# Twelve modulation blocks move from TensorE to VectorE, joined with a new order of work around them, in a two-layer encoder kernel

## What is computed

```python
for l in range(2):
    mod = c_act @ w_mod[l] + b_mod[l]          # (1024,) @ (1024, 6144)
    sh1, sc1, g1, sh2, sc2, g2 = split(mod, 6)
    h = rmsnorm(x, norm1_g[l]) * (1 + sc1) + sh1
    q, k, v, ca, cb, su, gates = split(h @ w_in[l])      # 5376 columns
    y_attn = sliding_window_attention(rope(q), rope(k), v) @ w_attn_o[l]
    y_conv = silu(layernorm(depthwise_conv31(ca * sigmoid(cb)))) @ conv_pw_w[l]
    y_ssm  = s5_ssm(su, ...)                   # (y @ glu_a) * sigmoid(y @ glu_b)
    mixed = gate_a * y_attn + gate_c * y_conv + gate_s * y_ssm
    x = x + g1 * (mixed @ w_out[l])
    h2 = rmsnorm(x, norm2_g[l]) * (1 + sc2) + sh2
    f_gate, f_up = split(h2 @ w_ffn_in[l])     # 2 x 2816 columns
    x = x + g2 * ((silu(f_gate) * f_up) @ w_ffn_out[l])
return rmsnorm(x, final_norm_g)
```

## Time and profile before

| | before |
|---|---|
| median of 3 runs (lowest, highest) | 977.05 us (977.03, 977.75) |
| the profiled execution's own time | 977.47 us |
| its span, first to last instruction | 975.6 us |
| TensorE busy | 926.7 us (95%) |
| VectorE busy | 669.4 us (69%) |
| ScalarE busy | 462.7 us (47%) |
| GpSimd busy | 9.4 us (1%) |
| mean granted TensorE clock | 0.990 |
| DMA, mean over the span | 201 GB/s |

### The profile page before, as it was taken

How to read it: one execution, slowest core, us unless ns; L and a number is a source line. 1 busy time by engine, 2 the same in 40 slices (tenths; PEclk the granted TensorE clock), 3 DMA queues, 4 the chain that set the end, 5 groups by cost and what they waited for, 6 DMA issues and landing times.

```text
span 975.6 us, 16235 instructions
## 1 busy us (share of the span) xinstructions
PE 926.7 (95%) x6917; PEld 783.7 (80%) x6917; DVE 669.4 (69%) x913; ACT 462.7 (47%) x540; POOL 9.4 (1%) x11
## 2 busy tenths in 40 slices
PE   5989999989999999999999999899999899999994
PEld 2888876667678888899989997567777799999994
DVE  4883999998567765473556758999947754444545
ACT  4684147624545565544445223574274544343432
POOL 2000000000000000000000000000000000000000
PEclk9999999999999999999999999899999999999998
DMA  8984356668696466566667334556869545555521
GB/s 356 237 266 138 112 187 215 216 183 306 268 283 216 153 224 223 199 210 230 209 173 210 120 106 173 179 190 192 297 228 331 180 173 195 174 189 199 173 87 43
DMA packets 128630, 196.13 MB, mean 201 GB/s; under 512 B 30793, under 2 KB 90705, under 8 KB 122415
## 3 DMA queue, kind: packets, MB, share of 16 engines
q1 hardware_dynamic: 128247, 195.03, 60.1%
q10 hardware_dynamic: 312, 0.08, 0.0%
HBM read 194.02 MB, written 1.06 MB: 200 GB/s over the span
## 4 chain that ended last, share of the span: by engine, by line
PE 53%; DVE 29%; ACT 7%; issue 5%; DMA 4%; SPq 2%; ACTq 0%; DVEq 0%
PE bank L569 15%; PE bank L570 15%; PE bank L571 15%; DVE wlo L1395 8%; DVE yc L1680 7%; DMA raw<-in_w_mod 3%; ACT whi L1062 3%; PE bank L607 2%; PE bank L665 2%; PE bank L832 1%; PE bank L689 1%; DVE blx L1653 1%; ACT h L1077 1%; DMA raw<-in_w_attn_o 1%; SPq L452 1%
## 5 line engine op out<-in xcount | busy, mean ns | idle before, releaser
L1395 DVE TENSOR_TENSOR wlo<-raw,whi 128x2048 fp32r<-128x2048 f32 (+1 forms) x135 | 302.8, 2243 | 219.6 <-PE bank L571 184.0
L1062 ACT ACTIVATE whi<-raw 128x2048 fp32r<-128x2048 f32 x132 | 252.2, 1911 | 111.7 <-PE bank L571 34.8
L569 PE MATMUL bank<-hhi,whi 128*128 128x256 f32 x928 | 265.6, 286 | 0.8 <-DVE wlo L1395 0.8
L570 PE MATMUL bank<-hlo,whi 128*128 128x256 f32 x928 | 262.6, 283 | 0.0
L571 PE MATMUL bank<-hhi,wlo 128*128 128x256 f32 x928 | 262.4, 283 | 0.0
L569 PEld LDWEIGHTS bank<-hhi,whi 128*128 128x128 f32 x928 | 177.8, 192 | 7.9 <-issue 5.0
L570 PEld LDWEIGHTS bank<-hlo,whi 128*128 128x128 f32 x928 | 177.9, 192 | 0.8 <-issue 0.2
L571 PEld LDWEIGHTS bank<-hhi,wlo 128*128 128x128 f32 x928 | 177.8, 192 | 0.0
L569 PE MATMUL bank<-whi,bhi 128*128 128x512 f32 x304 | 121.3, 399 | 1.9 <-DVE wlo L1395 1.9
L570 PE MATMUL bank<-wlo,bhi 128*128 128x512 f32 x304 | 118.8, 391 | 0.0
L571 PE MATMUL bank<-whi,blo 128*128 128x512 f32 x304 | 118.5, 390 | 0.0
(11 more groups left out here) (258 smaller groups left out, 885.6 us busy)
## 6 DMA issues: line engine op xcount, KB each, us to landing
raw<-in_w_mod SPq DMA_DIRECT2D x48, 1024.0 KB, 5.3
raw<-in_w_ffn_in SPq DMA_DIRECT2D x44, 1024.0 KB, 5.2
raw<-in_w_in SPq DMA_DIRECT2D x38, 1024.0 KB, 7.0
raw<-in_w_ffn_out SPq DMA_DIRECT2D x22, 1024.0 KB, 4.9
raw<-in_w_out SPq DMA_DIRECT2D x8, 1024.0 KB, 8.1
raw<-in_w_in SPq DMA_DIRECT2D x16, 256.0 KB, 4.5
raw<-in_ssm_glu_b SPq DMA_DIRECT2D x4, 1024.0 KB, 7.4
raw<-in_ssm_glu_a SPq DMA_DIRECT2D x4, 1024.0 KB, 6.1
```

The lines of the kernel that those rows point to most:

```text
L569: mm(o, w_hi, a_hi, start=start, stop=False, skip_group_check=True)
L570: mm(o, w_hi, a_lo, start=False, stop=False, skip_group_check=True)
L1062: fn(whi[mi % N_HI][:, :], raw[SLOT[item]][:, :], ACT.Copy).then_inc(s_hi, 1)
L1395: part = V.tensor_tensor(wlo[mi % N_LO][:, n], raw[SLOT[("main", *divmod(mi, NB))]][:, n], whi[mi % N_HI][:, n].bitcast(F32), ALU.subtract)
```

## The change

Five things are done together.

1. **Modulation.** Twelve of layer 1's blocks (group 0 and group 1, k = 2 to 7) are no longer multiplied by TensorE. VectorE multiplies the block by silu(c)[k] per partition and adds it up in `modacc` (the tensor `h`, 128 x 2048), in steps 41, 42, 43, 44, 46, 47 and 53, 56, 58, 59, 61, 62 of layer 0's FFN. TensorE sums `modacc` over the partitions with ones (`mod_sum`) in steps 49 and 64.
2. **From VectorE to ScalarE:** the scaling of the softmax (four instructions per group instead of one), the copy of v, the first tap of each pair of convolution channels, and the partial sums of the norms.
3. **New places:** v's turn at half step 20 (was 18), the rounding of the state-space output (`ssm_hi`) at z + 11, its remainder (`ssm_lo`) at z + 13 (both were z + 13), the convolution's pieces by a written list, layer 1's state-space input in two halves.
4. **Norms:** `wo`'s last tile is multiplied and added in two halves of 256 columns, x is updated without the sums and roots between the pieces, `lo` of the next blocks is cut in halves around it, and TensorE's turns, spreads and dummy matmuls stand in another order (34 dummies in all, 47 before).
5. **End:** GpSimd multiplies three of four pieces by final_norm_g and scales one of them; ScalarE scales two, VectorE one.

```diff
-SSM_IN_AT = [{8: STEP_TERMS[0:2], 9: STEP_TERMS[2:4], 10: STEP_TERMS[4:8]}, {Z_AT[1]: STEP_TERMS}]
+SSM_IN_AT = [{8: STEP_TERMS[0:2], 9: STEP_TERMS[2:4], 10: STEP_TERMS[4:8]}, {5: STEP_TERMS[0:4], 6: STEP_TERMS[4:8]}]
-SSM_SPLIT_AT = [z + 13 for z in Z_AT]
-ROPE_AT, V_TURN_AT = 17, 18
+SSM_HI_AT, SSM_LO_AT = [z + 11 for z in Z_AT], [z + 13 for z in Z_AT]
+ROPE_AT, V_TURN_AT = 17, 20
-CONV_AT = [{t0 + (43 - t0) * n // 15: divmod(n, 8) for n in range(16)} for t0 in (18, 15)]
+CONV_PIECES = [(19, 20, 22, 23, 25, 27, 28, 30, 31, 33, 35, 36, 38, 39, 41, 43), (14, 15, 19, 20, 22, 24, 26, 28, 30, 31, 33, 35, 37, 39, 41, 43)]
-MOD_AT[1] = {i: m for i, m in MOD_AT[0].items() if m[0] == 2 or m[1] >= NORM_MODS}
+MOD_AT[1] = {i: m for i, m in MOD_AT[0].items() if m[0] == 2}
-NEXT_MOD_AT = {PREP_AT + 2 + 4 * n: (0, NORM_MODS + n) for n in range(DK - NORM_MODS)}
+ACC_AT = {i: (1, ng, NORM_MODS + n) for ng, places in enumerate(((41, 42, 43, 44, 46, 47), (53, 56, 58, 59, 61, 62)))
+          for n, i in enumerate(places)}
+SUM_AT = {49: (1, 0), 64: (1, 1)}
+PIECES = [[(0, 0, 512), (0, 512, 1024), (1, 0, 512), (1, 512, 1024)],
+          [(0, 0, 512), (1, 0, 512), (0, 512, 1024), (1, 512, 768), (1, 768, 1024)]]
...
+            def mod_sum(l, ng):
+                pe.wait_ge(s_modacc, (DK - NORM_MODS) * (ng + 1))
+                if ng:
+                    pe.wait_ge(mod_ready, 3 * l + ng)
+                for q in range(4):
+                    last = mm(b_mod[32 * q:32 * q + 32, :], ones[:, 0:32], modacc[:, q * 512:(q + 1) * 512],
+                              start=(ng == 1), stop=(ng == 0), skip_group_check=True)
...
+            pool.wait_ge(s_final_g, 16)
+            for p in range(3):
+                t, c0, c1 = PIECES[0][p]
+                pool.wait_ge(*x_final(2 * DEPTH, p))
+                nc.gpsimd.tensor_tensor(gates[:, t, c0:c1], x[:, t, c0:c1], final_g[:, c0:c1], ALU.mult).then_inc(fin_pool, 1)
...
+            def softmax_scale(l, r):
+                act.wait_ge(den_ready, 4 * l + r + 1)
+                for t in range(4):
+                    last = fn(pr[:, t, :], pr[:, t, :], ACT.Copy, scale=rden[:, t:t + 1])
+                last.then_inc(pr_ready, 1)
...
+            def mod_accumulate(l, ng, k):
+                ...
+                if k == NORM_MODS:
+                    ...
+                    dve.wait_ge(landed, value)
+                    last = V.tensor_scalar(modacc, weights, w, None, ALU.mult)
+                else:
+                    dve.wait_ge(landed, value)
+                    dve.wait_ge(s_modacc, ACC_NO[item])
+                    last = V.scalar_tensor_tensor(out=modacc, in0=weights, scalar=w, in1=modacc, op0=ALU.mult, op1=ALU.add)
+                last.then_inc(s_modacc, 1)
...
                     post(l, i, (1,) if NAMES[i][0] in EARLY else (0, 1))
+                    for m3 in acc_at(l, i):
+                        mod_accumulate(*m3)
```

More of the change, by code:

```diff
@@ L229, with mod_no @@
 ITEMS, SLOT, LANDED, AFTER = plan_loads()
-MOD_ITEMS = [x for x in ITEMS if x[0] == "mod"]
-MOD_NO = {x: n for n, x in enumerate(MOD_ITEMS)}
+ACC_NO = {("mod", *m): n for n, m in enumerate(ACC_AT.values())}
+PE_MODS = [x for x in ITEMS if x[0] == "mod" and x not in ACC_NO]
+SUM_NO = [3 * DK + NORM_MODS + n for n in range(2)]
+def mod_no(item):
+    return PE_MODS.index(item) + sum(PE_MODS.index(item) >= 3 * DK + NORM_MODS for _ in SUM_NO)
+MOD_ENDS = [DK, 2 * DK, 3 * DK, SUM_NO[0] + 1, SUM_NO[1] + 1 + NORM_MODS, SUM_NO[1] + 1 + NORM_MODS + DK]
 LO_NO = {}
@@ L1009, in _ @@
                             mod_block(*m3)
+                    if l == 0 and i in SUM_AT:
+                        mod_sum(*SUM_AT[i])
                     side(l, 2 * i)
@@ L1262, in post @@
                 elif kind == "wo":
-                    if n % 2:
-                        for t in range(TILES):
-                            square(2 * l + 1, t, n // 2)
-                            if n == 3:
-                                root(2 * l + 1, t)
+                    for p in {1: (0, 1), 3: (2, 3, 4)}.get(n, ()):
+                        mean_square(2 * l + 1, p)
                 elif kind == "fu":
@@ L1281, in side @@
                     att_copy(l, ATTEND_AT[t])
+                if t == V_TURN_AT:
+                    v_copy(l)
+                if t in CONV_AT[l] and CONV_AT[l][t][1] == 0:
+                    conv_first(l, CONV_AT[l][t][0])
                 if t in SCORES_AT:
@@ L1312, in _ @@
             fn(cact[:, :], b_mod[:, 0:DK], ACT.Silu).then_inc(silu_c, 1)
-            for t in range(TILES):
-                for half in range(2):
-                    square(0, t, half)
-            for t in range(TILES):
-                root(0, t)
+            act.wait_ge(s_const, 32)
+            for p in range(4):
+                mean_square(0, p)
             prep(0)
@@ L1331, in _ @@
                     if i == NB - 1:
-                        for t in range(TILES):
-                            for half in range(2):
-                                square(2 * l + 2, t, half)
-                            root(2 * l + 2, t)
+                        for p in range(4):
+                            mean_square(2 * l + 2, p)
                     side(l, 2 * i + 1)
@@ L1850, in _ @@
             small_vectors_in(0)
-            for t in range(TILES):
-                part_sum(0, t)
             dve.wait_ge(s_const, 32)
```

275 lines of the change are left out of this document (158 added, 117 removed).

## The result

The changed kernel takes 962.4 us (median of 4 runs, 962.2 to 962.63) against 977.3: ratio 0.9847, 95% interval 0.983 to 0.9864. The forecast was 952.7. It is faster, by 14.9 us and not by 24.4. The profiled run has a span of 960.8 us.

A forecast was written before the change was run, and what follows sets the result against it. TensorE's work was taken as the bound. Terms -11.0 + 2.0 - 6.7 + 0 + 0.8 - 1.0 - 3.9 - 4.6 = -24.4 took 977.5 to 953.1, median 952.7; own range 946 to 959, 8 in 10 946 to 963.

The forecast's parts named there:

- modulation blocks and ring: Twelve blocks off TensorE at 1.10 us, two sums added: minus 11.0; late loads in layer 0's FFN four-buffer ring: plus 2.0.
- layer 1's mixer (softmax stall): TensorE's 4.47 us softmax wait shrinks to about 1.0 (minus 3.5) and the clock's fall behind it goes (minus 3.2): minus 6.7.
- layer 0's start and mixer: Under both mixers otherwise: VectorE's relief and ScalarE's added work cancel, 0, bounds minus 6 and plus 6 over both layers.
- two norms ahead of the FFN, `wo` halves: Narrower last piece of x in the norms, minus 1.0; `wo`'s matmuls of 256 columns in four blocks, plus 0.8.
- norm between the layers: Between the last `fo` block and layer 1: half a split, sums and root's wait leave VectorE, minus 3.9.
- the end: Kernel's end: sums and three products leave VectorE ahead of the last piece, one store leaves early: minus 4.6.
- rival A: Layer 1's mixer: the relief doesn't come because VectorE's order is late elsewhere; price 6.7 us, 959.4; chance 0.13.
- the ring at 5: Layer 0's FFN: late accumulations and loads in the four-buffer ring cost 5 us, against 2.0 taken and an upper bound of 6.
- Rival C: The clock falls in a norm, as 13 of 47 dummy matmuls are gone; 3.2 us per fall, 955.9 or 959.1; chance 0.09.
- three signs of being wrong: Waits for `wlo` growing beyond some 10 us, softmax stall standing as it was, GpSimd's product ending behind the last root.
- D: Layer 0's FFN: each of twelve accumulations delays the split behind it by 2.24, 26.9 us instead of 2.0, 977.6; chance 0.03.
- Rival B: Kernel's end: GpSimd's first product comes later than 2.6 us behind its input; cost 4.6 us, 957.3; chance 0.05.

The follow-up runs named there:

- E1: Changed kernel with all of layer 1's modulation blocks on TensorE again, the new order, norms and end kept: 962.7 us, ratio 0.9847.
- E10: E6 with the modulation block of step 37 multiplied by TensorE again: 954.5 us, ratio 0.9758.
- E6: E5 with the preparation product (b_source, steps 37 and 39) moved behind the step's own product: 953.7 us, ratio 0.9758.
- E5: Changed kernel with each accumulation ahead of the step's split in VectorE's queue instead of behind the product: 956.8 us, ratio 0.9788.
- E7: Changed kernel with the rounding of the state-space output (`ssm_hi`) two half steps later, where it stood before the change: 968.9 us, ratio 0.9903.
- E2: Changed kernel with the twelve accumulations reading x and their loads left out, so modulation values are wrong: 957.2 us, ratio 0.9781.
- E3: Changed kernel with accumulations over 64 columns instead of 2048, all loads in place, so modulation is wrong: 957.3 us, ratio 0.9791.
- E4: Changed kernel with group 0 of layer 1's modulation on TensorE again, only group 1 added up on VectorE: 963.1 us, ratio 0.9844.
- E8: Changed kernel with the end's three products by final_norm_g on VectorE again, GpSimd keeping only the scaling: 961.2 us, ratio 0.9827.
- E9: Kernel of before with the twelve accumulations and two sums alone, its order, norms and end kept: 979.6 us, ratio 1.0016.

## Why the prediction was right and where it was wrong

| term | forecast | measured |
|---|---|---|
| modulation blocks and ring | -11.0 + 2.0 = -9.0 | +0.8 (after against E1: +4.5, +0.4, -4.1) |
| layer 1's mixer (softmax stall) | -6.7 | -5.2 (E1) |
| layer 0's start and mixer | 0 | -3.2 (E1), -2.7 (after) |
| two norms ahead of the FFN, `wo` halves | -0.2 | -1.0 |
| norm between the layers | -3.9 | -3.7 (E1), -3.3 (after) |
| the end | -4.6 | -3.1 |

Without the modulation the sum was -15.4; E1 measured -15.7 by medians and -16.1 by spans. The direction is right, and the five terms besides the modulation are each off by 3.2 us at most. That their sum comes out within 0.7 is in part luck: the softmax stall and the end gave 1.5 us less each, and the two mixers otherwise, put at 0, gave 3.2 in layer 0. The total of 962.4 is inside the wider range (946 to 963) by 0.6 us and outside the forecast's own (946 to 959). The range's upper end stood for rival A with the ring at 5. A did not happen; what filled the gap was the modulation term, off by 9.8.

**The step that failed** is "Modulation blocks, minus 11.0", with its ring term. That a block costs TensorE 1.10 us is right where TensorE is never behind anyone: blocks 42 to 45 lost 1.1 to 1.2, 54 to 60 1.4 to 1.6. But the step took this price for all twelve (twelve removed, two sums added), on the view that TensorE is "all but always busy" in that FFN. Four things were missed:

1. *Blocks that filled a wait.* At step 37 TensorE waited for VectorE's split with the block and waits longer without (E10): 1.1 us. In layer 1's mixer 2.5 of 6.6 us do not show (E1). Of these 1.5 are longer softmax waits (0.86 in E1; 1.66 and 0.65 in the changed kernel), which the prediction had allowed for only inside the stall term; the rest was not traced.
2. *A wait that grew and took the clock along.* At block 41 TensorE came earlier to a round copy that is late for another reason (E6): 1.2 us, and 1.4 for the clock. Rival C's mechanism, in a place that the prediction did not look at, though the trace of before has the 1.15 us wait, at 358.80.
3. *The ring's way to TensorE.* The reckoning of a late load (end of the accumulation, issue, landing at up to 8.3, then `hi`) was right: 7.2 us from 373.87 to 381.04. (The terms of that reckoning, from block 42's end to block 46's split, add up to 19.0 us and not to the 18.7 written there; the trace has 18.6 from block 43's first matmul at 366.64 to the end of block 46's split at 385.27.) Its end was not. It went on to `lo` and block 46, but ScalarE's queue also carries the round copies, which TensorE needs half a block earlier. Two waits of 1.8 us and 4.1 us in all in blocks 45 to 48: more than the 2.0 taken, inside its bound of 6.
4. *The second group.* Another 1.2 us in blocks 60 to the end (E5 against after), which was taken as safe.

With 0.4 in the norm behind it this adds up: -11.0 + 1.1 + 2.5 + 2.6 + 4.1 + 1.2 + 0.4 = +0.9, against +0.8 measured.

None of the prediction's three signs of being wrong caught this. TensorE's waits for `wlo` are 6.0 us in all (5.4 before), the softmax stall did shrink, and GpSimd's last product ended at 954.30, before the last root. Of the rivals D is the nearest: the accumulations did fall on the path, in two places for some 5.3 us and not at every one of the twelve. C named a fall in a norm; the changed kernel has none there.

**The softmax stall** went as forecast in its mechanism: E7 undoes one number and has the stall and the clock's fall back. The wait is 1.66 where about 1.0 was forecast, and the clock stayed up in that run. In the eight profiled kernels with this same wait of 1.66, the clock fell behind it in four (E2, E3, E4, E6: 0.72 over 6 us in E6) and stayed at 1.00 in four (the changed kernel, E5, E8, E10). So that the 3.2 us for the clock came whole was in part luck of that run. Such falls fit the spread of single runs (E1's four are 961.4 twice, at a mean granted clock of 0.995 and 0.998, and 964.0 and 964.3 at 0.993), but no experiment isolated them.

**The end** missed by what GpSimd's three products and its scaling cost VectorE: four instructions at 1.23, 1.15, 1.07 and 1.06 instead of 0.69 are 1.75 us, enough for the whole miss of 1.5. Rival B, a late first product, did not come: the product at 949.21 starts 0.15 us behind the add that released it. The estimate of its duration, between 0.98 and twice that, held (1.27 to 1.29).

**The norm between the layers** is 0.4 short in the changed kernel, and alike in E4, E7 and E8, which have the same late accumulations of group 1; the kernels without them (E1), without their loads (E2), with short ones (E3) or with early ones (E5) have 6.2. So this too came from late accumulations at the FFN's end.

**Layer 0's mixer** was put at 0 and gained 3 us. The traces say where: from block 6 to block 21 it takes 122.3 to 122.4 us in each of the eleven kernels with the new order, and 125.8 in the two with the old one (before, E9). Three waits of TensorE in that stretch of before are gone, 0.92 at 165.57, 0.69 at 195.11 and 1.43 at 203.30, the last two for `wlo`. Which of the moves removed them was not tested. Blocks 0 to 5 vary from run to run: in E6's and E10's profiled executions the clock was down there twice, for 3.4 us each, and they take 59.6 and 59.9 us where the others take 57.0 to 58.6. So the mixer as a whole gained only 0.5 in these two.

E6 lies 24.5 us below its kernel of before, the changed kernel 14.9: 9.6 more, with the same work in better places. That this is the forecast's 24.4 is a coincidence, since the terms that make it up are others. What stays open: which move gave layer 0's mixer its 3 us, and whether the softmax waits of layer 1 can be removed instead of moved; padding them to hold the clock was not tried.

## What to carry to other kernels

A bound engine that is "99% busy" still has a few waits, and work taken from it can save nothing where it stands right ahead of one; look for the wait behind each removed piece before multiplying the price by the count. When an instruction holds a buffer of a ring, its place in its engine's queue matters more than its duration: put it where the engine waits anyway (E5 won 5.2 us of that FFN by order alone). And follow a late load through every instruction behind the waiting one in that queue, not only the one that the load is for.
